# Output norm, its first weights and the roles of the weight halves in a two-layer encoder

## The reference, cut to what matters

```python
for l in range(DEPTH):
    h = rms_norm(x, g_mix[l])
    proj = h @ w_in[l]
    ...
    o_a = dense_attention(qa, ka, kva[..., QK_NOPE:])
    ...
    o_b = dilated_sliding_attention(rope(pb[:, :, 0], pos), rope(pb[:, :, 1], pos), pb[:, :, 2])
    ...
    o_c = neighbourhood_attention(pc[:, :, 0], pc[:, :, 1], pc[:, :, 2], rpb[l])
    mixed = jnp.concatenate([
        rms_norm(o_a.reshape(b, s, WIDTH_A), out_norm_a[l]),
        rms_norm(o_b.reshape(b, s, WIDTH_B), out_norm_b[l]),
        rms_norm(o_c.reshape(b, s, WIDTH_C), out_norm_c[l]),
    ], axis=-1)
    x = x + mixed @ w_out[l]
    h2 = rms_norm(x, g_mlp[l])
    x = x + jnp.square(jax.nn.relu(h2 @ w_mlp_in[l])) @ w_mlp_out[l]
return rms_norm(x, g_final)
```

## Time and profile before

| | before |
|---|---|
| median of 3 executions | 2937.95 us (2937.46 to 2938.8) |
| profiled execution, its own time | 2937.11 us |
| its span, first to last instruction | 2935.0 us |
| PE matmul busy | 2854.4 us, 97% of the span |
| PE weight load busy | 2439.2 us, 83% |
| DVE busy | 1719.8 us, 59% |
| ACT busy | 1058.0 us, 36% |
| POOL busy | 141.7 us, 5% |
| mean granted TensorE clock | 0.991 |
| the chain that ended last, by engine | PE 86%, DVE 5%, issue 3%, DMA 3%, ACT 2% |

### The profile page before, as it was taken

One profiled execution on the slowest core, in us unless ns is written; L12 is line 12 of the kernel. 1 busy time (PEld: TensorE's weight loads), 2 busy tenths in 40 slices (PEclk: granted clock), 3 DMA queues, 4 the chain that ended last, 5 costly groups with the idle time before them and its releaser, 6 DMA issues.

```text
span 2935.0 us, 39902 instructions
## 1 busy us (share of the span) xinstructions
PE 2854.4 (97%) x14640; PEld 2439.2 (83%) x14640; DVE 1719.8 (59%) x2998; ACT 1058.0 (36%) x1976; POOL 141.7 (5%) x253
## 2 busy tenths in 40 slices
PE   7999999989999999999999999999899999999998
PEld 7898888878888888888798978888788888888887
DVE  5641777875555455455666337788655455455457
ACT  5332777874311111111244237778632111111113
POOL 0000330000000000000000012300000000000000
PEclk9999999999999999999999999999999999999999
DMA  5656884313111111111146577743221111111111
GB/s 195 183 188 156 199 192 113 88 43 115 43 44 57 43 43 57 43 43 64 45 176 205 168 191 179 178 101 87 67 78 43 43 57 43 43 57 43 43 62 69
DMA packets 182359, 285.34 MB, mean 97 GB/s; under 512 B 48848, under 2 KB 138576, under 8 KB 172496
## 3 DMA queue, kind: packets, MB, share of 16 engines
q1 hardware_dynamic: 171600, 254.16, 29.7%
q0 software_dynamic: 10624, 29.41, 3.6%
HBM read 210.60 MB, written 72.88 MB: 97 GB/s over the span
## 4 chain that ended last, share of the span: by engine, by line
PE 86%; DVE 5%; issue 3%; DMA 3%; ACT 2%; DVEq 1%; SPq 0%; ACTq 0%; POOLq 0%
PE ps L1407 24%; PE ps L1233 20%; PE ps L1422 18%; PE ps L1306 7%; PE ps L1320 6%; PE ps L1352 6%; PE ps L1362 2%; PE ps L1201 1%; DMA biasC<-in_bias_c 1%; DMA values<-vst 1%; PE ps L1270 1%; PE ps L1345 1%; DVE x L1154 1%; DVE hn L908 1%; DVE vbuf L1141 1%
## 5 line engine op out<-in xcount | busy, mean ns | idle before, releaser
L1422 PE MATMUL ps<-w_dn,hid 128*128 128x512 f32 x3072 | 713.6, 391 | 1.4
L1407 PE MATMUL ps<-hT,w_up 128*128 128x512 f32 x3072 | 702.5, 389 | 3.3 <-DVE hT L891 3.3
L1422 PEld LDWEIGHTS ps<-w_dn,hid 128*128 128x128 f32 x3072 | 573.6, 188 | 132.5 <-DVE x L1154 14.0
L1407 PEld LDWEIGHTS ps<-hT,w_up 128*128 128x128 f32 x3072 | 576.2, 188 | 123.1 <-ACT rbuf L841 3.7
L1233 PE MATMUL ps<-ws,hT 128*128 128x384 f32 (+3 forms) x3072 | 607.7, 356 | 3.1 <-issue 1.6
L1233 PEld LDWEIGHTS ps<-ws,hT 128*128 128x128 f32 x3072 | 535.1, 190 | 50.3 <-DVE ws L891 2.7
L1154 DVE TENSOR_TENSOR x<-ps,x 128x512 f32<-128x512 f32 x512 | 342.9, 689 | 223.9 <-PE ps L1422 223.7
L1141 DVE TENSOR_TENSOR vbuf<-rbuf 128x512 f32<-128x512 f32 x128 | 88.6, 692 | 371.0 <-ACT rbuf L841 371.0
L792 ACT ACTIVATE pT<-ps 128x512 fp32r<-128x512 f32 (+1 forms) x448 | 240.5, 582 | 141.5 <-PE ps L1320 139.6
L891 DVE TENSOR_TENSOR pT<-ps,pT 128x512 fp32r<-128x512 f32 (+1 forms) x448 | 281.4, 664 | 6.9 <-ACT pT L792 5.8
L841 ACT ACTIVATE rbuf<-ps 128x512 f32<-128x512 f32 x128 | 76.6, 598 | 553.9 <-PE ps L1407 553.9
(11 more groups left out here) (85 smaller groups left out, 2140.8 us busy)
## 6 DMA issues: line engine op xcount, KB each, us to landing
raw<-in_wstream SPq DMA_DIRECT2D x76, 1024.0 KB, 4.9
head<-feats SPq DMA_DIRECT2D x192, 256.0 KB, 6.3
feats<-tst SPq DMA_DIRECT2D x128, 192.0 KB, 2.6
values<-vst POOLq DMA_DIRECT2D x32, 384.0 KB, 3.2
head<-values SPq DMA_DIRECT2D x24, 512.0 KB, 4.0
biasC<-in_bias_c SPq DMA_DIRECT2D x16, 768.0 KB, 12.3
raw<-in_wstream SPq DMA_DIRECT2D x12, 768.0 KB, 5.8
x_park<-x SPq DMA_DIRECT2D x16, 512.0 KB, 9.5
```

The lines of the kernel that those rows point to most:

```text
L1407: last = pe.matmul(ps[:, k % 2, :], w_up[0 if first else 1][:, w1, kt, ft * P:(ft + 1) * P], hT[:, w2, kt, sh * 512:(sh + 1) * 512], start ...
L1422: last = pe.matmul(ps[:, 2 + m % 4, :], hid[slot][:, w1, ft, s * P:(s + 1) * P], w_dn[1 if last_group else 0][:, w2, ft, nh * 512:(nh + 1) ...
```

## The change

Three things change.

- **Order at the end of the attention.** On ACT, the two units of `o0` are split right after the copy of block 30, then come the sums of tile 0, then the copy of block 31 (before the sums of tile 1); the wait for all blocks moves down to tile 4, and ahead of tile 0 there is a wait for the first 31 only. On DVE, the first half of `o0` is split after the division of block 30; then tile 0 is scaled, the second half split, the rest of tile 0 made, tile 1 scaled, and only then block 31 divided. On PE, `merge(31)` writes to bank 4 in place of bank 7. The first projection is cut in two: twelve matmuls with the first half of the features, then the turn of tile 1, then the other twelve; the turn of tile 2 follows.
- **Half of `o0`.** `SLOT` puts `o0` in half 1 and `o1` in half 0, so that `o0` shares memory with the second last head and not with the last.
- **Roles by layer.** All that lies in the two halves takes its half from `slot_of(l, k) = (k + l) % 2`, and the MLP's buffers change places, so that what follows `o0` and `o1` finds its half free. `kR`, `prob`, `oT` and `biasC1` exist once for each role.

```diff
-SLOT = {job: (j if j < NJ - 2 else j - NJ + 2) % 2 for j, job in enumerate(JOBS)}
+SLOT = {job: (j if j < NJ - 2 else j - NJ + 1) % 2 for j, job in enumerate(JOBS)}
...
-    kR = sb("kR", [P, SEQ], f32r, "WS", 52 * KB)
-    prob = sb("prob", [P, 2, 1024], f32, "WS", 20 * KB)
-    oT = sb("oT", [P, 1024], f32, "WS", 28 * KB)
+    kR = [sb(f"kR{k}", [P, SEQ], f32r, "WS", (52 - 32 * k) * KB) for k in range(2)]
+    prob = [sb(f"prob{k}", [P, 2, 1024], f32, "WS", (20 + 32 * k) * KB) for k in range(2)]
+    oT = [sb(f"oT{k}", [P, 1024], f32, "WS", (28 + 32 * k) * KB) for k in range(2)]
...
+        def slot_of(l, k):
+
+            return (k + l) % 2
...
+        def merged(b):
+
+            return ps[:, 4 if b == NB - 1 else 6 + b % 2, 0:4 * HD]
...
                     for b in blocks_at(i):
-                        act.wait_ge(pv_done, l * NB + b + 1)
-                        if b >= 2:
-                            act.wait_ge(mg_done, l * NB + b - 1)
-                        act.activation(oT[:, (b % 2) * 512:(b % 2 + 1) * 512], ps[:, 6 + b % 2, :], ACT.Copy)\
-                           .then_inc(ot_ready, 1)
-                act.wait_ge(o_ready, (l + 1) * NB)
+                        if b < NB - 1:
+                            copy_sum(b)
+                act.wait_ge(pv_done, l * NB + NB - 2)
+                split_job(l, "o0", 0)
+                split_job(l, "o0", 1)
+                act.wait_ge(o_ready, l * NB + NB - 1)
                 act.wait_ge(grid_back, (l + 1) * HC * 16)
 
                 def output_weights(t):
-                    if t == 2:
-                        split_job(l, "o0", 0)
-                        split_job(l, "o0", 1)
-                    elif t in (4, 5):
+                    if t == 1:
+                        copy_sum(NB - 1)
+                    if t == 4:
+                        act.wait_ge(o_ready, (l + 1) * NB)
+                    if t in (4, 5):
                         split_job(l, "o1", t - 4)
...
+                        if b < NB - 1:
+                            output(b)
+                split_job(l, "o0", 0)
...
-                    if t == 2:
-                        split_job(l, "o0", 0)
-                        split_job(l, "o0", 1)
...
-                norm(l, ST, O, [(0, HA * HD), (HA * HD, (HA + HB) * HD), ((HA + HB) * HD, DM)], 1, between)
+                groups = [(0, HA * HD), (HA * HD, (HA + HB) * HD), ((HA + HB) * HD, DM)]
+                dve.wait_ge(gain_in, (l * 3 + 2) * 16)
+                norm_scale(l, ST, 0, O, groups)
+                split_job(l, "o0", 1)
+                norm_lo(l, ST, 0)
+                norm_scale(l, ST, 1, O, groups)
+                output(NB - 1)
+                for t in range(2, ST + 1):
+                    between(t)
+                    if t < ST:
+                        norm_scale(l, ST, t, O, groups)
+                    norm_lo(l, ST, t - 1)
...
                 norm_turn(l, ST, 0)
+                pe.wait_ge(nt_free, l * TN + 2 * (ST + 1) + 2)
+                project(l, acc, "o0", 0, (0, KT // 2))
                 norm_turn(l, ST, 1)
-                for s in range(ST):
+                project(l, acc, "o0", 0, (KT // 2, KT))
+                norm_turn(l, ST, 2)
+                for s in range(1, ST):
                     pe.wait_ge(nt_free, l * TN + 2 * (ST + s + 1) + 2)
-                    project(l, acc, "o0", s)
-                    acc += 1
+                    project(l, acc + s, "o0", s)
                     if s + 2 < ST:
                         norm_turn(l, ST, s + 2)
+                acc += ST
```

More of the change, by code:

```diff
@@ L1031, in _, with output @@
                         turn += 1
+                def output(b):
+                    kind, h, q = ITEMS[4 * b]
+                    if b == 0:
+                        for k in range(NTS):
+                            dve.wait_ge(tst_out[k], (l + 1) * 16 * TST_N[k])
+                        for k in range(2):
+                            dve.wait_ge(vst_out[k], (l + 1) * 16 * (len(VSTAGED) // 2))
+                    dve.wait_ge(mg_done, l * NB + b + 1)
+                    o = O[:, q:q + 4, h * HD:(h + 1) * HD]
+                    if kind == "C":
+                        o = oC[h % 2][:, q:q + 4, :]
+                        done = l * HC + h - HA - HB - 1
+                        if done > 0:
+                            dve.wait_ge(grid_parked, done * 8 * 16)
+                    dve.reciprocal(a_rd[:, 4 * b:4 * b + 4], a_den[:, 4 * b:4 * b + 4])
+                    dve.drain()
+                    dve.tensor_tensor(o, merged(b).rearrange("p (t d) -> p t d", d=HD),
+                                      a_rd[:, 4 * b:4 * b + 4].unsqueeze(2).to_broadcast([P, 4, HD]),
+                                      ALU.mult).then_inc(o_ready, 1)
                 for i in range(STEPS):
@@ L1067, in _ @@
                     for b in blocks_at(i - 3):
[L1068 to L1084, removed]
-                                          ALU.mult).then_inc(o_ready, 1)
+                        if b < NB - 1:
+                            output(b)
+                split_job(l, "o0", 0)
                 acc = len(ACCS) - 2 * ST
@@ L1223, in project @@
                     for w1, w2 in PASSES:
[L1224 removed]
+                        for (kt, _), (_, wv) in zip(up_views(l, kind, w1), up_views(l, kind, w2)):
                             mms.append((latT[:, s % 2, w1, kt, :], wv))
                 else:
[L1227 removed]
+                    for kt in range(*kts):
                         for w1, w2 in PASSES:
[L1229 removed]
+                            mms.append((hT[:, w1, kt, s * P:(s + 1) * P], w_view(l, job, w2)[:, kt, :]))
+                n0 = len(PASSES) * kts[0]
                 for n, (a, b) in enumerate(mms):
[L1231 removed]
+                    if s == 0 and job != "up" and n0 + n == len(PASSES) * KT // 2:
                         pe.wait_ge(split_lo, l * NU + unit_of(job, 1) + 1 + 2)
[L1233 to L1234 removed]
+                    last = pe.matmul(out_, a, b, start=(n0 + n == 0),
+                                     stop=(n == len(mms) - 1 and kts[1] == KT))
+                if kts[1] == KT:
+                    last.then_inc(acc_done, 1)
             for t in range(LEAD):
@@ L1361, in merge @@
                         c = k * P + (b % 2) * 512
-                        last = pe.matmul(ps[:, 6 + b % 2, k * HD:(k + 1) * HD], oT[:, c:c + P], pair[:, :],
+                        last = pe.matmul(merged(b)[:, k * HD:(k + 1) * HD], oT[l % 2][:, c:c + P], pair[:, :],
                                          start=True, stop=True)
@@ L1406, in up @@
                                 for w1, w2 in PASSES:
-                                    last = pe.matmul(ps[:, k % 2, :], w_up[0 if first else 1][:, w1, kt, ft * P:(ft + 1) * P],
+                                    last = pe.matmul(ps[:, k % 2, :], w_up[slot_of(l, 1 if first else 0)][:, w1, kt, ft * P:(ft + 1) * P],
                                                      hT[:, w2, kt, sh * 512:(sh + 1) * 512],
```

108 lines of the change are left out of this document (55 added, 53 removed).

## The result

| | before | after |
|---|---|---|
| median | 2938.38 us (2937.46 to 2941.57, 4 executions) | 2923.11 us (2918.54 to 2928.63, 4 executions) |
| ratio | | 0.9948, 95% interval 0.9936 to 0.9959 |
| profiled execution | 2937.11 us | 2928.63 us |
| span | 2935.0 us | 2926.6 us |
| mean granted clock | 0.991 | 0.993 |

The changed kernel is 15.3 us faster, and 2922.5 us had been forecast. The profiled execution of the changed kernel is the slowest of its four and shows only 8.5 us of that (2937.11 - 2928.63).

A forecast was written before the change was run, and what follows sets the result against it. PE, multiplying for 97% of the span, was taken as the bound, with time to win where it waits at each attention's end. 2937.95 - 15.45 (7.75 + 7.7 for the layers) = 2922.5 us; range 2918.0 to 2927.0.

The forecast's parts named there:

- Yardstick: Start of the projection's tile 1, 671.65 us in layer 0: whatever makes it earlier is kept to the layer's end.
- ACT's splits and block 31: End of attention, ACT: two splits take 3.71 us after block 30's copy; block 31's copy moves 0.5 us later, costing nothing further.
- The twelve matmuls: First half of projection tile 0 on PE: starts at 655.0 us, 7.8 us earlier, after a 2.9 us wait.
- ACT and DVE's loop behind it: Work on tiles 1 and 2: at full clock projection tile 1 starts at 662.5 us, gaining 9.15 us in layer 0.
- The clock: PE's 2.9 us wait before the projection: clock falls in each layer, 1.65 us lost, tile 1 starts at 663.9 us.
- The long stretch of 6.8 us: Rival with a longer slow stretch at the first projection: 3.83 us lost, gain 5.6 us a layer, 2926.8 us; chance 0.14.
- rival 1: Clock holds at one or both waits before the projection: 2921.1 us with one fall, 2919.7 with none; chance 0.37.
- a limit near 2.4 us: PE waits elsewhere in the old trace: 2.42 us passed at full clock, six of six from 2.46 us on fell.
- Roles by layer: Buffers' halves flipped by layer: same instructions and bytes at other addresses, no effect, bound 0.5 us either way.
- Rival 3: End of attention: splits move but tile 0's norm does not; 2.3 us a layer, 2933.3 us; chance 0.06.
- Rival 4: First projection tiles: the clock doesn't come back; with four slow tiles 16 us a layer lost, 2970 us; chance 0.03.
- The sum: Both layers' ends of attention: gain 7.75 + 7.7 = 15.45 us, taken from the median 2937.95 us.

The follow-up runs named there:

- after_filled: The changed kernel with ten further matmuls of 512 columns on TensorE behind the turn of tile 0, into unread bank 5; 2920.12 us, 0.9937.
- after_p3: A further single profiled execution of the changed kernel, nothing altered; 2922.16 us.
- whole_first: The changed kernel with the first projection in one piece of 24 matmuls and the turns of tiles 1 and 2 behind it; 2927.01 us, 0.996.
- splits_early: The kernel before with only the two units of `o0` split early and the memory roles this needs; 2933.26 us, 0.9982.
- after_again: The changed kernel run once more, nothing altered, with a second profile; 2926.89 us, 0.9958 against the kernel before on the same chip.

## Why the prediction was right, step by step

- **Yardstick.** The start of the projection's tile 1 carries to the end of the layer: right. TensorE has no gap behind it, and the end of layer 1 follows at 816.7 us in both kernels.
- **ACT's splits and block 31.** The splits took 3.71 us, as in the earlier trace rows, and block 31's copy came 5.88 us after block 30's, where 6.3 had been worked out and 5.76 was before. The wait before `merge(31)` is 0.77 us.
- **The twelve matmuls** were to start 12.06 us after the copy of block 30 (655.0) and started at 11.70, in every profile of this order. The 0.36 us are hand-overs on ACT, where instructions in a row overlap by some 0.1 us each. The wait in front was to be 2.9 us and is 2.64.
- **ACT and DVE's loop behind it.** At full clock tile 1 was to start at 19.32 us in the timeline (662.5 in the chain, less 0.24), and started at 19.06 in after_filled and after_p3. So 9.15 us was the right size of the full gain (28.20 - 19.06 = 9.1 measured).
- **The clock.** A fall in each passage was forecast, with 1.65 us lost on TensorE and 1.4 us net. It fell in seven of eight passages of the changed kernel. The net cost was 1.2 to 1.5 us in three of them, as forecast, and 2.4 to 2.8 us in four. The long stretch of 6.8 us is the term that was too small: I gave it 0.14, and it came in half the passages. My price for it, 3.5 us net, was too high: the turn behind the twelve lost 0.1 to 0.5 us (the next twelve start 0.91 to 1.25 us behind it, 0.79 at full clock), where 1.1 us had been counted, and the twelve lost 2.45 us (5.49 - 3.04), where 2.73 had been counted.
- **The Trainium skill's rule** ("TensorE: Matmul & The Clock Gate", section "What's actually happening", that the point of a change of clock differs from run to run) holds here: one wait of 2.64 us was passed at full clock in after_p3, layer 1, and in whole_first, layer 1, and not in layer 0 of the same executions. That was rival 1, at 0.37; in the profiles the clock held in one passage of eight. What stood against rival 1, a limit near 2.4 us, is not a limit either: in after a wait of 2.33 us in layer 0 went with a fall, and one of the same length at 1755.56 us in layer 1 was passed at full clock. The timeline of PE and a stretch, after, layer 0:

```profile
126.19 0.87 PE L1304 MATMUL ps<-ident,stage 128*128 128x128 f32 x3 [2.33 <-ACTq L744]
...
126.00:127.00 1.00, 0.81 (x4) 0.84 (x5) 0.29 (x1) 0.84 (x3) 0.00 (x0) 0.50 0.17 50
```

- **Roles by layer** at nothing: right (1.0 [0.9991, 1.0009]). **Rival 3** did not occur in the whole kernel. Its price, 2.3 us a layer, is what splits_early measured (2.4 and 2.1), but by luck: the price rests on the reading that TensorE waited for `o0` from 660.5 to 662.81. It turned tile 1 from 660.06 to 662.00 and stood idle for only 0.81 us. splits_early started 1.26 us earlier, and the rest came from the clock. **Rival 4** did not occur: the clock was never low for more than 6.8 us in the changed kernel's passages.
- **The sum.** 7.75 us a layer was forecast and 7.3 us is the mean of the passages. Twice 7.3 is 14.6 us, and the two comparisons gave 15.3 and 11.8 us (after_again). What the sum lacked is all that differs outside the passages: 1.4 us up to the first and 4.0 us between them in the profiled execution, which was 5.5 us slower than the median. The prediction's sentence that TensorE would be gapless "from there on" holds for the rest of the layer, not for the front of layer 1. The range of 2918.0 to 2927.0 holds both medians of the changed kernel, but it was drawn for the low clock and the hand-overs and not for this. That 2922.5 and the first median, 2923.11, are so close is in part luck: the second median, 2926.89, lies 4.4 us above the forecast and 0.1 us inside the range. What the runs bear out is the mechanism, through the passages: 7.3 us a layer for 7.75.

## What to carry to other kernels

Where a chain over several engines stands between two dense stages, ask which outputs of the last step the next one needs first: here four of eight tiles did not need the last block, two of them were moved ahead of it, and with the weights prepared in the same wait this gave 7.3 us a layer where the moves alone gave 2.3 and 2.8. Such moves are to be priced together, and memory has to be arranged for them first, which costs and gives nothing by itself. What is left of the wait still lowers TensorE's clock; idle TensorE time of known length, filled with matmuls into an unused bank, brought another 6.8 us against the same kernel on the same chip, 3.6 us of it in the passages.

## What the runs showed of the hardware

- Ten matmuls nobody needs, in a wait of 2.64 us, keep the granted clock at 1.00 and make the kernel faster (0.9937 against 0.9958 on the same chip). In the kernel before, 40 of them do (0.9984).
- The same wait in the same program lets the clock fall or not, and the low stretch lasted 3.4 or 6.8 us in the changed kernel, 10.2 us with one move alone, and 13.7 us before. The length of the wait alone does not decide: in one execution of the changed kernel a wait of 2.33 us went with a fall and another of 2.33 us did not.
- Executions of one kernel differ by 6 us (2935.38 to 2941.1 in 21 of before on one chip). Two parts of it are seen: at what waits the clock falls, and a store in layer 1 for which ScalarE waits 3.4 to 8.4 us and TensorE then stands between 0.3 and 5.6 us. Where ScalarE waited over 8 us (six of fourteen profiles), SP had taken 2.4 to 2.5 us to issue one store. Why it did is open.
